# Projections of three attention branches rewritten as three fp32r products, and scores taken over 64 rows instead of zero-padded queries

## What is computed

```
proj = h @ w_in                         # dilated: q, k, v of 3 groups x 8 heads x 64
s_h  = q_h @ k_h.T * 64**-0.5           # per head, contraction over 64
p_h  = softmax(s_h - distance * slope); o_h = p_h @ v_h
mod  = silu(c) @ ada_w + ada_b          # 6 x 1024 values per layer
```

## Time and profile before

| | us |
|---|---|
| median of 3 runs (3066.44 to 3071.8) | 3068.12 |
| the profiled execution | 3062.41 |
| its span, first to last instruction | 3061.1 |
| PE busy in it | 2708.2 (88%) |
| DVE / ACT / POOL busy | 1222.5 / 845.7 / 511.7 |
| TensorE clock granted, mean | 0.932 of 2.4 GHz |

### The profile page before, as it was taken

The page is one execution under the profiler, slowest core; times in us unless marked ns, Lnnn a source line. Parts: engine busy times, 40 slices in busy tenths (PEclk is TensorE's granted clock), DMA queues, the critical chain, the costliest instruction groups (busy, mean ns, idle before and its releaser), DMA issues. The chain is left out here.

```text
span 3061.1 us, 34956 instructions
## 1 busy us (share of the span) xinstructions
PE 2708.2 (88%) x13844; PEld 2142.3 (70%) x13844; DVE 1222.5 (40%) x2216; ACT 845.7 (28%) x1672; POOL 511.7 (17%) x595
## 2 busy tenths in 40 slices
PE   6999968689869999399899899997898899799997
PEld 5898958476555555286667687875697796587886
DVE  5533152242231111400553666525574563433333
ACT  2323231342121111110463321223422322332222
POOL 4564714300012222120000100001020110100001
PEclk9999978799979999699999899998998899899999
DMA  6332400002338999420001466522102102232322
GB/s 216 124 108 86 137 16 27 11 28 85 87 138 325 402 418 373 172 69 28 1 1 56 139 184 197 167 69 77 35 1 56 28 1 56 83 90 79 108 81 71
DMA packets 325649, 338.84 MB, mean 111 GB/s; under 512 B 19120, under 2 KB 296752, under 8 KB 313072
## 3 DMA queue, kind: packets, MB, share of 16 engines
q1 hardware_dynamic: 303280, 279.69, 27.8%
q0 software_dynamic: 22208, 56.93, 5.2%
HBM read 370.11 MB, written 16.78 MB: 126 GB/s over the span
## 5 line engine op out<-in xcount | busy, mean ns | idle before, releaser
L331 DVE TENSOR_TENSOR sb_w_lo<-sb_weights,sb_w_hi 128x1024 fp32r<-128x1024 f32 (+2 forms) x215 | 239.9, 1125 | 503.4 <-ACT sb_w_hi L325 503.2
L373 PE MATMUL bank<-sb_h_hi,sb_w_hi 128*128 128x512 f32 x1040 | 421.0, 405 | 11.6 <-DVE sb_w_lo L331 11.6
L375 PE MATMUL bank<-sb_h_hi,sb_w_lo 128*128 128x512 f32 x1040 | 408.4, 393 | 0.0
L374 PE MATMUL bank<-sb_h_lo,sb_w_hi 128*128 128x512 f32 x1040 | 407.9, 392 | 0.0
L325 ACT CAST sb_w_hi<-sb_weights 128x1024 fp32r<-128x1024 f32 x224 | 215.5, 970 | 554.4 <-PE bank L375 489.1
L414 POOL TENSOR_TENSOR sb_scratch<-sb_scratch 128x512 f32<-128x512 f32 x30 | 38.7, 1288 | 1320.5 <-ACT sb_scratch L404 1320.5
L913 PE MATMUL bank<-sb_weights,sb_hT 128*128 128x256 f32 x960 | 233.7, 400 | 14.2 <-DVE sb_padded L1361 12.3
L373 PEld LDWEIGHTS bank<-sb_h_hi,sb_w_hi 128*128 128x128 f32 x1040 | 196.8, 189 | 65.7 <-issue 25.7
L913 PEld LDWEIGHTS bank<-sb_weights,sb_hT 128*128 128x128 f32 x960 | 214.1, 286 | 23.6 <-issue 13.1
L374 PEld LDWEIGHTS bank<-sb_h_lo,sb_w_hi 128*128 128x128 f32 x1040 | 197.0, 189 | 45.6 <-issue 5.3
L375 PEld LDWEIGHTS bank<-sb_h_hi,sb_w_lo 128*128 128x128 f32 x1040 | 196.6, 189 | 43.2
(11 more groups left out here) (488 smaller groups left out, 4947.1 us busy)
## 6 DMA issues: line engine op xcount, KB each, us to landing
sb_weights<-ffn_w_in SPq DMA_DIRECT2D x88, 512.0 KB
sb_mod_weights<-ada_w POOLq DMA_DIRECT2D x24, 1024.0 KB, 5.6
sb_weights<-ada_w SPq DMA_DIRECT2D x24, 1024.0 KB
sb_expert_weights<-w_down SPq DMA_DIRECT2D x17, 1024.0 KB
sb_weights<-w_in SPq DMA_DIRECT2D x16, 1024.0 KB
sb_weights<-ffn_w_out SPq DMA_DIRECT2D x32, 512.0 KB
sb_weights<-gdn_w_in SPq DMA_DIRECT2D x32, 512.0 KB
sb_expert_weights<-w_up SPq DMA_DIRECT2D x14, 1024.0 KB
```

The costliest lines, as they stand in the source:

```text
L331: dve.tensor_tensor(u.lo[:, 0:u.kt, :], u.chunk.w, u.hi[:, 0:u.kt, :].bitcast(F32), ALU.subtract).then_inc(*k.lo.one())
L373: pe.matmul(bank[:], u.hi[:, kk, :], act[0][:, kk, :], start=first and kk == 0, stop=False)
L374: pe.matmul(bank[:], u.hi[:, kk, :], act[1][:, kk, :], start=False, stop=False)
L375: mm = pe.matmul(bank[:], u.lo[:, kk, :], act[0][:, kk, :], start=False, stop=last and kk == u.kt - 1)
```

## The change

It replaces the float32 projections of the dilated, latent and head-group stages by blocks of two contraction tiles by 512 (384, 288) columns, each split into high and low halves in three buffers `wide`, with three fp32r matmuls per contraction tile and token tile. `first_norm` and `block_norm` now write the normed activations as a pair `k.h`. The first two blocks of a stage are split ahead of it (low halves on POOL, `block_lo_pool`), the others inside it (ACT, then DVE, `block_lo_dve`). The padding of queries is gone: scores contract 64 rows (`head_rows`). PE's modulation turns move from the projections to the first four steps of the dilated attention; the modulation loads go into `xT`, which SP reads back from memory at the start of `merge`. `merge` no longer splits `hT`. The extra weight slots of these stages are gone.

```diff
+def head_rows(h):
+    return slice(h % 2 * HD, (h % 2 + 1) * HD)
...
+def block_hi_act(k, b, free=None):
+    act = k.nc.scalar
+    act.wait_ge(*b.chunk.ready)
+    if free:
+        act.wait_ge(*free)
+    act.copy(b.hi, b.chunk.w).then_inc(*k.block_hi.one())
...
+def block_lo_dve(k, b):
+    dve.wait_ge(*b.hi_ready)
+    dve.tensor_tensor(b.lo, b.chunk.w, b.hi.bitcast(F32), ALU.subtract).then_inc(*k.block_lo.one())
...
+def block_rows_pe(k, b, kk, bank, tokens, last):
+    pe, (hi, lo), r = k.nc.tensor, k.h, b.k0 + kk
+    out = bank[:, 0:b.n]
+    pe.matmul(out, hi[:, r, tokens], b.hi[:, kk, :], start=r == 0, stop=False)
+    pe.matmul(out, hi[:, r, tokens], b.lo[:, kk, :], start=False, stop=False)
+    return pe.matmul(out, lo[:, r, tokens], b.hi[:, kk, :], start=False, stop=last)
...
 def first_norm(k, gain, arrived, blocks):
     norm_root_act(k, k.summed.at(KD))
-    norm_rows_dve(k, gain, None, None)
-    k.meet()
+    block_hi_act(k, blocks[0])
+    block_lo_pool(k, blocks[0])
+    block_hi_act(k, blocks[1])
+    block_lo_pool(k, blocks[1])
+    norm_shift_act(k, None, k.h)
+    norm_rows_dve(k, gain, None, k.h)
...
 def attention_pe(k, jobs, normalise, pieces=()):
-            if padded and j.h == 0:
-                pe.wait_ge(*k.padded_even.at(j.tile + 1))
-                pe.wait_ge(*k.padded_odd.at(j.tile + 1))
             mm = pe.matmul(bank[:, 0:j.n], j.query, j.keys, start=True, stop=not j.bias)
...
+        for p in pieces[2 * s:2 * s + 2]:
+            modulation_pe(k, p)
...
 def modulation_pool(k, pieces):
         if p.i == 0:
+            pool.wait_ge(*k.h_rows.last())
             modulation_load_pool(k, p)
...
-        if p.i >= 2:
-            pool.wait_ge(k.mod_turned.sem, p.i - 1)
...
 def dilated_project_act(k, g, blocks, q, kt, v):
+    for t in range(48 + 1):
+        if t % 4 == 0 and t // 4 + 2 < 12:
+            block_hi_act(k, blocks[t // 4 + 2], block_done(k, t // 4 - 1) if t else None)
...
 def dilated(k, plans, after):
-                jobs.append(Job(i, h, k.padded[i % 2][:, h, :], kt[:, h // 2, lo * P:(i + 1) * P],
+                jobs.append(Job(i, h, q[head_rows(h), h // 2, i * P:(i + 1) * P],
+                                kt[head_rows(h), h // 2, lo * P:(i + 1) * P],
...
+        modulation_add_dve(k, 0, 16 * g, 16)
+        for b in following[:2]:
+            block_lo_pool(k, b)
         k.meet()
...
 def open_scores(k):
-    k.padded = [k.sb(f"padded{i}", [P, H, P]) for i in range(2)]
-    k.more_weights(more)
-    for tile in k.padded:
-        k.nc.vector.memset(tile[:], 0.0).then_inc(*k.dve_step.one())
-    k.meet()
+    wide = k.sb("wide", [P, 6, 1024], F32R)
+    k.wide = [(wide[:, 2 * i, :], wide[:, 2 * i + 1, :]) for i in range(3)]
...
 def merge(k):
-    split_rows_act(k, h, k.hT)
-    split_rows_dve(k, h, k.hT)
+    for mark in marks:
+        k.nc.sync.wait_ge(*mark)
+    for kk in range(KD):
+        k.nc.sync.dma_start(k.xT[:, kk, :], k.io["xT"][kk * P:(kk + 1) * P, :]).then_inc(back, 16)
...
 def stick_pe(k, qb, kb, vb, o):
-                pe.matmul(k.bank[j][:, 0:S - j * P], kb[:, h // 2, j * P:(j + 1) * P], padded[:, h, j * P:S],
+                pe.matmul(k.bank[j][:, 0:S - j * P], kb[head_rows(h), h // 2, j * P:(j + 1) * P], qb[head_rows(h), h // 2, j * P:S],
...
-                pe.matmul(bank[:, 0:n], kb[:, h // 2, i * P:(i + 1) * P], padded[:, h, i * P:S], start=True, stop=False)
+                pe.matmul(bank[:, 0:n], kb[head_rows(h), h // 2, i * P:(i + 1) * P],
+                          qb[head_rows(h), h // 2, i * P:S], start=True, stop=False)
...
 def head_groups(k, blocks, wide):
-    pad_queries(k, qb, padded)
-    stick_pe(k, padded, kb, vb, o)
+    stick_pe(k, qb, kb, vb, o)
```

More of the change, by code:

```diff
@@ L550, in __init__, with attention_pe @@
         self.n = keys.shape[-1]
-def attention_pe(k, jobs, padded, normalise):
+def attention_pe(k, jobs, normalise, pieces=()):
     pe = k.nc.tensor
@@ L767, in modulation_end_dve @@
     out = k.mod[:, layer, :, :]
-    dve.wait_ge(*k.mod_turned.last())
-    dve.tensor_tensor(out.rearrange("p s k -> p (s k)"), k.bank[7][:, 0:6 * KD], k.ada_b[:, layer, :], ALU.add
-                      ).then_inc(*k.dve_step.one())
     dve.wait_ge(*k.dve_step.last())
@@ new lines, in dilated_project_dve @@
+def dilated_project_dve(k, blocks, other):
+    dve = k.nc.vector
+    for t in range(48):
+        n = ended(t - 1)
+        if n is not None and n < 8:
+            head_sum_dve(k, n, DIL_H, HD)
+        n = ended(t - 2)
+        if n is not None and n < 8:
+            if n >= 4:
+                dve.wait_ge(*k.turned.at(n - 3))
+            head_scale_dve(k, n, heads_of(k.bank[n][:], DIL_H), DIL_H, HD, heads_of(k.scr[3 + n % 4][:], DIL_H))
+        if t % 4 == 1 and t // 4 + 2 < 12:
+            block_lo_dve(k, blocks[t // 4 + 2])
+        if t % 2 == 0:
+            next(other, None)
@@ L975, in dilated @@
+    for p, after_next in zip(all_pieces, all_pieces[2:] + [None, None]):
+        p.later = after_next
     other = angles_dve(k)
@@ L988, in dilated @@
             angles_act(k)
-        load_weights_sp(k, chunks)
+        load_weights_sp(k, [b.chunk for b in blocks])
         modulation_pool(k, pieces)
@@ new lines, in mla_query_dve @@
+def mla_query_dve(k, blocks):
+    dve = k.nc.vector
+    for t in range(32 + 2):
+        n = ended(t - 1)
+        if n is not None:
+            head_sum_dve(k, n, 4, MLA_D)
+        n = ended(t - 2)
+        if n is not None:
+            if n >= 4:
+                dve.wait_ge(*k.turned.at(n - 3))
+            head_scale_dve(k, n, heads_of(k.bank[n][:, 0:4 * MLA_D], 4), 4, MLA_D,
+                           heads_of(k.scr[3 + n % 4][:, 0:4 * MLA_D], 4))
+        if t < 32 and t % 4 == 1:
+            block_lo_dve(k, blocks[t // 4 + 2])
@@ new lines, in groups_project_pe @@
+    first_blocks_pe(k, blocks[:4], k.bank[0:4], tokens)
+    for t in range(16, 64):
+        b, i = t // 4, t % 4
+        if b >= 8 and b % 4 == 0:
+            pe.wait_ge(*k.dve_copied.at(NT * (b // 4 - 2) + i + 1))
+        block_pe(k, blocks[b], i, k.bank[b // 4 % 2 * 4 + i], tokens(i))
+        n = ended(t - 8)
+        if n is not None and n < 8:
+            pe.wait_ge(*k.roped.at(n + 1))
+            for j in range(4):
+                mm = pe.transpose(k.bank[n][:, j * P:(j + 1) * P], k.scr[n % 4][:, j * P:(j + 1) * P], k.const("ident"))
+            mm.then_inc(*k.turned.one())
@@ new lines, in groups_project_act @@
+def groups_project_act(k, blocks, va, qb, kb, vb):
+    act = k.nc.scalar
+    for t in range(64 + 32 + 1):
+        if t % 4 == 0 and t // 4 + 2 < 24:
+            block_hi_act(k, blocks[t // 4 + 2], groups_done(k, t // 4 - 1) if t else None)
+        n = ended(t - 1) if t <= 64 else None
+        if n is not None:
+            act.wait_ge(*k.projected.at(n + 1))
+            if n < 8:
+                if n >= 4:
+                    act.wait_ge(*k.turned.at(n - 3))
+                act.copy(k.scr[n % 4][:], k.bank[n][:]).then_inc(*k.shifted.one())
+            else:
+                act.copy((va, vb)[n // 4 - 2][:, n % 4, :], k.bank[n % 8][:]).then_inc(*k.shifted.one())
+        if t > 64 and t % 4 == 0:
+            m = t // 4 - 17
+            act.wait_ge(*k.projected.at(16 + m + 1))
+            act.activation((qb, kb)[m // 4][:, m % 4, :], k.bank[m][:], ACT.Copy, scale=1.0 if m < 4 else HD ** -0.5
+                           ).then_inc(*k.shifted.one())
```

545 lines of the change are left out of this document (259 added, 286 removed).

## The result

The changed kernel is slower: 3142.95 us, median of 4 runs (3109.59 to 3145.79), against 3067.28 (3062.16 to 3071.8), a ratio of 1.022 with a 95% interval of 1.015 to 1.029. The interval is wide because one run took 3109.59 at a mean granted clock of 0.892, the others 0.881; the runs' records do not say in which stage it differed. The forecast was 3046, in a range of 3008 to 3076: wrong sign, and outside the range.

The account below looks back on a forecast made before the run. PE was taken to set the rewritten projections, with POOL next. Dilated -3.5, latent -8, merge +5 and head groups -15.5 gave -22 on the median 3068.1, so 3046 us, range 3008 to 3076.

Parts of the forecast that it names:

- the price is per change between 128 and 64 rows: Attention scores: entering and leaving a 64-row group costs 0.40 us together; 32 pairs of changes per attention, 12.8 us.
- +13, +7, +7 and +12: Added us from 64-row scores in the attentions of dilated groups 0, 1 and 2 and the causal attention.
- the slower one: Rival 3, dilated projections: low halves on DVE get in once per POOL piece; +35 us, 3081; chance 0.10.
- head groups: Head groups' projection: fp32r triples replace float32 records on PE, 136 us against 170.7, -34.5.
- latent: Latent branch, 80.1 us before: 17.5 us less on PE, half of it taken, -8; bounds 0 and -17.
- the dilated groups: Projections of dilated groups 1 and 2: end when POOL ends, 100.1 to 86 us, -14 each.
- The mechanism of POOL and DVE: Dilated projections: two-operand SBUF instructions on DVE and POOL exclude each other; ten low halves lengthen POOL's chain 11 us, to 86.
- The rival of the starved DVE: Rival 3, dilated projections: one low half per POOL piece, 101 us instead of 86 in groups 1 and 2; chance 0.10.
- group 0: Dilated projection of group 0: ends at 126.5 us against 128.9, -2.5, with PE idle from about 105.
- `merge`: Start of `merge`: eight `xT` loads go ahead of the weights, so PE starts 13 us after the attention, +5.
- Stick-breaking: Stick-breaking attention: 32 pairs of row changes at 0.40 us, +13; `pad_queries` goes, -4.
- The rival of two row tiles at once: Rival 4, 64-row scores: they cost half their records and changes cost nothing; 2970 us; chance 0.03.

Follow-up runs that it names:

- the probe: Kernel before, plus blocks of matmuls alone on PE between causal attention and stick-breaking, each behind 50 128-row matmuls; all at clock 1.00, 0.38 us per pair of changes.
- e13_filler: Changed kernel plus 128-row filler matmuls in the causal attention, six ahead of the first score and one behind each of the first eight; 3104.86 us.
- e1: Changed kernel with zero-padded queries back in the dilated and causal attentions, stick-breaking scores still over 64 rows; 3010.39 us, ratio to before 0.982.
- e8: Changed kernel with all scores padded, 7 of 24 modulation pieces moved into the dilated attentions, and `xT` loads issued ahead of the latent attention; 2979.89 us.
- e12_probe_cold: Matmul blocks alone on PE, each behind a pause of some 10 us, so starting at the lower clock; 64-row blocks stayed low for 102 and 107 us.
- e6: Changed kernel with padded queries back in the dilated and causal attentions and the stick-breaking scores padded as well; 3012.06 us (one run).
- e5: Changed kernel, scores still over 64 rows, with the scores of two jobs, an even and an odd head, side by side on PE; 3034.17 us.

## Why the prediction was wrong

The step that failed is in the part on scores over 64 rows: "the price is per change between 128 and 64 rows", and with it the sums +13, +7, +7 and +12 for the four attentions, together 39. They measured 41 + 26 + 26 + 64 = 157 (first score to last record; in the causal attention 54.5 became 118.3). The price itself was right, 0.38 us in the probe against 0.40. What was missing is that it is a price at the full clock, and that the clock need not be full. I read 0.93 to 1.00 before and carried it over, though the change halves the rows of every score. None of the five rivals had a lower clock in it; the slower one put 35 us on POOL and DVE. The four terms are 118 us short, more than the whole miss of 3143 - 3046 = 97.

How much of the 118 is the clock is measured for the causal attention: with all its changes it takes about 65 us at the full clock (e13_filler, less its fillings) and 118.3 at half, so 53 of its 64 us are the clock, and the other 10 are the changes, for which 12 were forecast. For the three dilated attentions no run has 64-row scores at the full clock. That their 93 us are mostly the clock as well is argued from the column of the clock, 0.50 throughout, and from e1, which gave most of them back at clocks of 0.76 to 0.87.

Point by point:
- *Projections.* Right: the terms for head groups (-34.5, measured 138.0 against 136), latent (-8, measured -5.2) and the dilated groups (86 each, measured 83.7 and 80.5). The mechanism of POOL and DVE held too, though its size was too large: POOL's eight pieces took 83.2 and 80.4 us from the first product to the last sum, where seven times 9.43 and one of 8.2 would have been 74.2, so the low halves lengthened the chain by 9 and 6 us and not by 11. In the timeline of POOL, a piece beside a low half and the last one, with DVE idle:

```profile
226.47 3.62 POOL L805 TENSOR_TENSOR sb_xT<-sb_xT,sb_cond 128x2048 f32<-128x2048 f32 x1
230.16 4.61 POOL L809 TENSOR_TENSOR sb_xT<-sb_xT 128x1024 f32<-128x1024 f32 x2
...
283.51 3.68 POOL L809 TENSOR_TENSOR sb_xT<-sb_xT 128x1024 f32<-128x1024 f32 x2
```

  0.93 us longer, the length of most of a low half; and the low half beside it on DVE takes 5.39 instead of 1.23:

```profile
225.79 5.39 DVE L373 TENSOR_TENSOR sb_wide<-sb_weights,sb_wide 128x1024 fp32r<-128x1024 f32 x1
```

  PE then stood 7.1 us behind POOL's last sum ahead of the attention of group 1. The rival of the starved DVE did not come: inside that projection PE waited 2.5 us for DVE's head norms and not for a low half. In group 0 the end was right (125.4 against 126.5) and the way to it partly luck: POOL ended the stage, but PE was at work until 121.6 and not until about 105, since it had waited 13.7 us in the midst of the stage for DVE's head norms, which were not in the sum.
- *`merge`.* Right, 14.3 against 13. e8 confirms the cause, the eight `xT` loads ahead of the first weights.
- *Stick-breaking.* Too dear: +8.8 with the pads' 3.7 gone, so +5 net, forecast +9. The stage began at 0.50 for 16.5 us and came back by itself, beside eight records over 128 rows and 512 to 128 columns in a row (L2425, from 1614.3 us; the clock is 0.65 in the window 1616 to 1618 and 1.00 behind it). That these brought it back fits e12_probe_cold and was not tested. With padded scores (e6) it took 3.4 us less, pads included; that the other changes hide where PE waits is argued, not shown.
- *The rival of two row tiles at once* had 0.03. The chip does it, but not in this order of scores: an even and an odd head never stood side by side. In e5 they did.
